# Experts ranked by token count, and two of eight positions cut from 96 to 64 token slots

## The reference, cut to what matters

```
logits = x @ router_w + router_b
top_v, top_i = top_k(logits, 2);  top_p = softmax(top_v)
out = sum over e of gate[:, e] * ((silu(x @ w1[e]) * (x @ w3[e])) @ w2[e])
```

## Time and profile before

| | us |
|---|---|
| median of 3 runs (2125.89 to 2126.81) | 2125.93 |
| span of the profiled execution, first to last instruction | 2121.4 |
| median less the profile's span | 4.5 |
| PE busy in the span | 2007.0 (95%) |
| DVE, ACT, POOL busy | 745.1, 593.2, 53.8 |
| HBM read | 614.43 MB |

### The profile page before, as it was taken

One profiled execution on the slowest core, in us unless ns is written; L12 is line 12 of the kernel. 1 busy time (PEld: TensorE's weight loads), 2 busy tenths in 40 slices (PEclk: granted clock), 3 DMA queues, 4 the chain that ended last, 5 costly groups with the idle time before them and its releaser, 6 DMA issues.

```text
span 2121.4 us, 38539 instructions
## 1 busy us (share of the span) xinstructions
PE 2007.0 (95%) x17128; PEld 1242.4 (59%) x17128; DVE 745.1 (35%) x1325; ACT 593.2 (28%) x972; POOL 53.8 (3%) x96
## 2 busy tenths in 40 slices
PE   9999999987978879999999999999999999999997
PEld 7778874322422237877888877745556554344445
DVE  8775663110100117786444677610001000000015
ACT  6555541000100016565444755400000000000005
POOL 1000000000000000120000002000000000000000
PEclk9999999999999999999999999999999999999999
DMA  9854468999999997254555551389999999999991
GB/s 220 205 157 140 158 218 333 421 421 421 421 421 421 421 408 232 80 169 159 178 181 196 162 178 42 134 309 405 409 412 405 372 405 407 412 409 409 411 409 73
DMA packets 239199, 622.96 MB, mean 294 GB/s; under 512 B 35496, under 2 KB 120360, under 8 KB 201648
## 3 DMA queue, kind: packets, MB, share of 16 engines
q1 hardware_dynamic: 233872, 611.87, 77.0%
q10 hardware_dynamic: 4544, 6.42, 0.8%
q0 software_dynamic: 608, 2.10, 0.3%
HBM read 614.43 MB, written 3.81 MB: 291 GB/s over the span
## 4 chain that ended last, share of the span: by engine, by line
PE 75%; DMA 15%; DVE 5%; ACT 2%; issue 1%; SPq 0%; POOL 0%; DVEq 0%; ACTq 0%; POOLq 0%
PE ps L2840 21%; PE ps L2857 11%; DMA ring<-in_w_gate 8%; DMA ring<-in_w_down 5%; PE ps L664 5%; PE ps L666 5%; PE ps L665 5%; PE ps L2546 4%; PE ps L674 2%; PE ps L675 2%; PE ps L678 2%; PE ps L2561 2%; DMA arena<-in_w_gate 1%; DMA arena<-in_w_down 1%; PE ps L2135 1%
## 5 line engine op out<-in xcount | busy, mean ns | idle before, releaser
L2840 PE MATMUL ps<-ring,arena 128*32 128x512 f32 (+1 forms) x3936 | 395.2, 557 | 0.0
L704 DVE TENSOR_TENSOR ring_parts<-ring,high_parts 128x2048 fp32r<-128x2048 f32 (+2 forms) x117 | 261.9, 2244 | 93.9 <-ACT high_parts L700 93.0
L2840 PEld LDWEIGHTS ps<-ring,arena 128*32 128x32 f32 x3936 | 148.1, 110 | 230.1 <-issue 204.8
L3053 DVE TENSOR_TENSOR arena<-ps,arena 128x768 f32<-128x768 f32 (+1 forms) x24 | 21.4, 891 | 601.6 <-ACT arena L2956 537.5
L700 ACT CAST high_parts<-ring 128x2048 fp32r<-128x2048 f32 (+2 forms) x117 | 217.5, 1862 | 31.7 <-PE ps L666 28.4
L666 PE MATMUL ps<-high_parts,arena_parts 128*128 128x512 f32 (+1 forms) x494 | 194.3, 393 | 0.0
L664 PE MATMUL ps<-high_parts,hT_parts 128*128 128x512 f32 (+1 forms) x472 | 191.6, 406 | 0.0
L665 PE MATMUL ps<-ring_parts,hT_parts 128*128 128x512 f32 (+1 forms) x472 | 185.1, 392 | 0.0
L2857 PE MATMUL ps<-ring,arena 128*32 128x256 f32 x3168 | 176.1, 379 | 0.0
L2956 ACT ACTIVATE arena<-ps,arena 128x256 f32<-128x256 f32 (+1 forms) x72 | 27.6, 454 | 511.8 <-PE ps L2840 511.7
L2546 PE MATMUL ps<-ring,arena 128*64 128x512 f32 x584 | 145.0, 596 | 21.8 <-DMA ring<-in_w_gate 11.9
(11 more groups left out here) (650 smaller groups left out, 2502.7 us busy)
## 6 DMA issues: line engine op xcount, KB each, us to landing
ring<-in_moe_w SPq DMA_DIRECT2D x220, 512.0 KB, 10.0
ring<-in_moe_w SPq DMA_DIRECT2D x66, 1024.0 KB, 12.0
ring<-in_moe_w SPq DMA_DIRECT2D x108, 384.0 KB, 8.2
ring<-in_w_gate SPq DMA_DIRECT2D x39, 1024.0 KB, 27.6
ring<-in_w_down SPq DMA_DIRECT2D x35, 1024.0 KB, 27.6
ring<-in_w_up SPq DMA_DIRECT2D x34, 1024.0 KB, 27.6
ring<-in_w_in SPq DMA_DIRECT2D x104, 256.0 KB, 4.6
arena<-in_w_up SPq DMA_DIRECT2D x26, 1024.0 KB, 26.4
```

The source lines that it names most:

```text
L704: dve.tensor_tensor(low_flat(p), raw_flat(p), f32(high_flat(p)), ALU.subtract).then_inc(split, 1)
L2840: mm = pe.matmul(dst, x_rows, w[:, :, s * n:(s + 1) * n], start=(c == 0), stop=(c == KC - 1), skip_group_check=True)
```

## The change

The experts are ranked by token count on the chip. Expert 0 keeps position 0 and is given rank 1, since its weights are loaded before the router is done. The seven others are put in the other positions by their rank: position 2 takes the second fewest (rank 7), position 7 the fewest (rank 8), and both compute two lots (64 slots) in place of three. The second path is taken when an expert has more tokens than its own slots.

DVE makes the order in a small one-hot matrix `o_turn`, and everything by expert (places, gates) is turned into position order with it. SP waits for `expert_order` before the first piece of position 1, loads the expert's number into a register once for each position, and addresses all weights of positions 1 to 7 by that register.

```diff
 LOTS, SPAN = 3, 96
+LOTS_AT, RANK_AT = (3, 3, 2, 3, 3, 3, 3, 2), (1, 2, 7, 3, 4, 5, 6, 8)
+ROWS_AT_POS = [32 * sum(LOTS_AT[:k]) for k in range(len(LOTS_AT))]
+        def stream_ranked(sp, pieces):
+            expert = {}
+            for p in pieces:
+                if p.free_at:
+                    sp.wait_ge(used, p.free_at)
+                elif p.slot == RAW + 1:
+                    sp.wait_ge(sig("router_psum"), 3)
+                if p.bucket not in expert and p.bucket:
+                    if not expert:
+                        sp.wait_ge(*ended("expert_order"))
+                    at = p.bucket
+                    expert[at] = sp.value_load(order_i[0:1, at:at + 1], min_val=0, max_val=NE2 - 1)
+                sources = p.source(bass.ds(expert[p.bucket], 1)) if p.bucket else [src for _, src in p.copies]
+                for (dst, _), src in zip(p.copies, sources):
+                    sp.dma_start(dst, src).then_inc(piece_ready[p.slot], 16)
...
+        def rank_key_dve(dve):
+            dve.tensor_copy(o_key_base[:], desc[:, 32 - NE2:32])
+            dve.tensor_copy(o_rank_at[:], slot_no[:, 0:NE2])
+            dve.drain()
+            dve.memset(o_key_base[:, 0:1], BIG)
+            for at, r in enumerate(RANK_AT):
+                if r != at + 1:
+                    ins = dve.memset(o_rank_at[:, at:at + 1], float(r))
+            vstep(dve, ins)
+        def ranked_place_dve(dve):
+            upto, total = router_psum(moe2)
+            place = r_place[:, :, 0:NE2]
+            dve.wait_ge(sig("router_psum"), 2 * moe2.number)
+            dve.tensor_copy(place[:, 1], total[:, 0, :])
+            dve.tensor_tensor(place[:, 0], upto[:, 0, :], r_hit[:, 0, 0:NE2], ALU.mult)
+            vstep(dve, dve.scalar_tensor_tensor(out=o_key[:], in0=total[:, 0, :], scalar=float(NE2), in1=o_key_base[:], op0=ALU.mult, op1=ALU.add))
+            dve.tensor_tensor(place[:, 1], place[:, 1], upto[:, 1, :], ALU.add)
+            vstep(dve, dve.scalar_tensor_tensor(out=o_key[:], in0=total[:, 1, :], scalar=float(NE2), in1=o_key[:], op0=ALU.mult, op1=ALU.add))
+            dve.tensor_tensor(place[:, 1], place[:, 1], r_hit[:, 1, 0:NE2], ALU.mult)
+            vstep(dve, dve.tensor_tensor(o_pairs, ..., ALU.is_ge))
+            vstep(dve, dve.tensor_reduce(o_rank[:], o_pairs, AX, ALU.add))
+            vstep(dve, dve.tensor_tensor(o_turn[:], ..., ALU.is_equal))
+            ranked(dve, o_place, place)
+        def ranked(dve, dst, src):
+            for t in range(NT):
+                ins = dve.tensor_tensor(o_wide[:, t], o_turn[:], src[:, t].unsqueeze(1).to_broadcast([P, NE2, NE2]), ALU.mult)
+            vstep(dve, ins)
+            vstep(dve, dve.tensor_reduce(dst, o_wide, AX, ALU.add))
+        def expert_order_dve(dve):
+            ...   (six steps; the fourth signals expert_order, the last two make o_cap, 96 or 64 for each expert)
...
         def router2_dve(dve):
             lower_rows_dve(dve, moe2, 1)
+            rank_key_dve(dve)
             dve.wait_ge(sig("router_psum"), 3)
...
-            place_dve(dve, moe2)
+            ranked_place_dve(dve)
         def gates2_dve(dve):
             yield from two_gates(dve, moe2, NE2)
+            ranked(dve, o_gate[:, :, :, 0], ...)
+            dve.tensor_copy(o_gate[:, :, :, 1], ...).then_inc(sig("moe2_gates"), 1)
...
             def up(st, c):
-                for g in range(LOTS):
+                for g in range(st.lots):
             def down(st, i):
-                    for g in range(LOTS):
+                    for g in range(st.lots):
             def result(b):
-                for g in range(LOTS):
+                for g in range(n):
             def last_result():
-                    for g in range(LOTS):
+                    for g in range(LOTS_AT[b]):
             def silu(st):
-                for g in range(LOTS):
+                for g in range(st.lots):
             def product(st):
-                hid, hidT = wide_hid[:, 0:LOTS * n], wide_hidT[st.no % 2][:, 0:LOTS * n]
+                hid, hidT = wide_hid[:, 0:lots * n], wide_hidT[st.no % 2][:, 0:lots * n]
...
             select(0)
             rows(0)
             hot_kept()
+            expert_order_dve(dve)
             all_of(gates2_dve(dve))
             count_dve(dve, f)
```

More of the change, by code:

```diff
@@ L76 @@
 LOTS, SPAN = 3, 96
+LOTS_AT, RANK_AT = (3, 3, 2, 3, 3, 3, 3, 2), (1, 2, 7, 3, 4, 5, 6, 8)
+LAST = 32 * LOTS_AT[-1]
+ROWS_AT_POS = [32 * sum(LOTS_AT[:k]) for k in range(len(LOTS_AT))]
+FEW = min(r for r, n in zip(RANK_AT, LOTS_AT) if n < LOTS)
+assert all((n < LOTS) == (r >= FEW) for r, n in zip(RANK_AT, LOTS_AT)) and RANK_AT[0] == 1
 PIECE = 2048
@@ L437, in plan_wide @@
                     st.first, st.last = k == 0, c0 + st.n == DFF
+                    st.lots = LOTS_AT[b]
                     f.plan.append(st)
             def down(st):
-                rows = w2[st.bucket][st.c0:st.c0 + st.n].rearrange("(p c) n -> p c n", p=P)
-                return [new_piece([(0, PIECE, rows[:, c:c + 2, :])]) for c in range(0, st.n // P, 2)]
+                rows = w2[0][st.c0:st.c0 + st.n].rearrange("(p c) n -> p c n", p=P)
+                lot = []
+                for c in range(0, st.n // P, 2):
+                    p = new_piece([(0, PIECE, rows[:, c:c + 2, :])])
+                    p.source = lambda e, c0=st.c0, n=st.n, c=c: [
+                        w2[e].rearrange("a n d -> (a n) d")[c0:c0 + n].rearrange("(p c) n -> p c n", p=P)[:, c:c + 2, :]]
+                    p.bucket = st.bucket
+                    lot.append(p)
+                return lot
             slot_flat[RAW:RAW + 2] = [arena[:, WIDE_SLOT:WIDE_SLOT + PIECE], hT[:].rearrange("p c s -> p (c s)")]
@@ L614, in stream_moe @@
                 lot = [p for st in f.plan for pair in st.up + st.down for p in pair]
+                stream(sp, sorted(lot, key=lambda p: p.n))
             else:
                 lot = [p for st in f.plan for p in st.up] + [p for st in f.plan for p in st.down]
-            stream(sp, sorted(lot, key=lambda p: p.n))
+                stream_ranked(sp, sorted(lot, key=lambda p: p.n))
             sp.wait_ge(sig("routed"), 2 * f.number)
@@ L1863, in count_dve @@
             vstep(dve, dve.tensor_tensor(r_count[:, 0:nb], r_count[:, 0:nb], total[:, 1, :], ALU.add))
+            if f is moe2:
+                for at in range(NE2):
+                    dve.memset(o_row_at[:, at:at + 1], float(ROWS_AT_POS[at] - 1 - ROWS_AT_POS[-1]))
+                vstep(dve, dve.tensor_tensor(r_count[:, 0:nb], r_count[:, 0:nb], o_cap[:], ALU.subtract))
+                vstep(dve, dve.tensor_scalar(r_count[:, 0:nb], r_count[:, 0:nb], float(f.cap), float(S), ALU.add, ALU.min))
             vstep(dve, dve.tensor_reduce(r_count[:, 0:1], r_count[:, 0:nb], AX, ALU.max))
@@ L1919, in two_gates @@
                 ins = dve.tensor_tensor(gate[:, t, :, 0:f.e], first, second, ALU.add)
-            ins.then_inc(sig(f"{f.name}_gates"), 1)
+            if f is moe1:
+                ins.then_inc(sig("moe1_gates"), 1)
+            else:
+                vstep(dve, ins)
         def logits_dve(dve, n, bias):
@@ L2859, in down @@
                                            stop=(st.last and j == st.n // P - 1), skip_group_check=True)
-                            if final and (k, g, s) == (1, LOTS - 1, 1):
+                            if final and (k, g, s) == (1, st.lots - 1, 1):
                                 mm.then_inc(sig("moe2_half_done"), 1)
@@ L3151, in rest_dve @@
                     places = r_place[:, :, 0:f.subs]
-                    dve.tensor_scalar(places, places, -float(P if k else f.cap), None, ALU.add).then_inc(m("shifted"), 1)
+                    if f is moe2 and k == 0:
+                        dve.tensor_tensor(places, places, o_cap[:].unsqueeze(1).to_broadcast([P, NT, NE2]), ALU.subtract).then_inc(m("shifted"), 1)
+                    else:
+                        dve.tensor_scalar(places, places, -float(P if k else f.cap), None, ALU.add).then_inc(m("shifted"), 1)
                     dve.wait_ge(*m.at("shifted", k + 1))
```

85 lines of the change are left out of this document (57 added, 28 removed).

## The result

The changed kernel takes 2112.97 us (median of 4 runs, 2110.49 to 2113.52) where the kernel before takes 2125.91 beside it: ratio 0.9939, 95% interval 0.9925 to 0.9953, 12.9 us less. In a second set of runs it took 2114.66 (4 runs) against 2125.03: 0.9948, 0.9931 to 0.9964. The prediction was 8.0 us less, 2117.9. Both medians lie in its range (2112 to 2124); the second lies 0.3 us and the first 2.0 us under the band that it called its forecast (2115 to 2121).

A forecast was written before the change was run, and what follows sets the result against it. PE and the DMAs were both taken as full, the DMAs' lead over PE deciding. Stage -11.1, start +2.5 and branch +0.6 gave -8.0 us: span 2113.4, time 2117.9 with 4.5 around it; range 2112 to 2124.

The forecast's parts named there:

- The bound: Expert stage: PE needs 85.2 us per 96-slot position and the transfers about the same, so both are full.
- The lead, piece by piece: Weights lie ready 12.7 us early at position 2, eaten after some 15 pieces; second gather returns 6 to 8 us.
- The stage, -11.1: Expert stage: lead at the end 5.4, shorter last piece 0.9, fuller queue 4.5, smaller result 0.3 us off.
- The slow stretch: 1640 to 1720, after the second gather: 379 instead of 410 GB/s, 6.0 us lost, 4.5 expected back.
- The start, +2.5: Router to first gather: added DVE steps, 1.6 us for places and 0.9 for keys; bounds 1.5 and 5.
- The branch, +0.6: PE's branch at the stage's end fetches code by DMA behind four queued pieces: 0.6 us longer, bounds 0 and 1.25.
- Gates, order, SP, next stage at nothing: Added gate and order steps hidden, SP's DMAs by register short enough, next stage's weights not late: 0 us.
- The two rules weighed: Skill rules on clock falling to 1.2 GHz in PE pauses (0.84 us here) and on DMA limits, 358 and 435 GB/s.
- rival 4: Clock falls in positions 2 and 7, two-lot piece 3.4 us against 2.56 of DMA: 2119 to 2121; chance 0.24 with another rival.
- The rate: Weight stream at 410 GB/s: by the fabric ceiling of 435 it could still speed up by 6%.

The follow-up runs named there:

- the control: The kernel before itself, unchanged, run again beside the others: 2125.99 us (10 runs), ratio to before 1.0002.

## Why the prediction was right, and where its sizes were off

- **The bound.** Both full, the lead decides: right. With a full queue every trace shows 405 to 413 GB/s over stretches of 60 us and more, whatever PE does; stretches of 20 us go from 391 to 416 in the two traces of the changed kernel.
- **The lead, piece by piece.** Issue, landing and use of every piece stand in the trace of the changed kernel. The lead is 12.6 us where position 2 begins (12.7 forecast) and is gone after 14 pieces of two lots (some 15). The second gather gives back 7.3 us (6 to 8). One step of the path failed: that lead was to last until position 7, for positions 3 to 6 were taken as even. The stream needs 86.1 us for each of them (the first pieces of positions 3 and 7 land at 1622.80 and 1967.10), PE 85.1, so 1.5 us are left when position 7 begins, and PE waits from its second piece on. The sum doesn't feel it, since it takes the whole lead at the end as gone either way. It fits that position 7, cut on top of position 2, adds only 2.6 us of stage.
- **The sum, in the traces.** The first pair is the trace of before and the first of the changed kernel, the second pair the control and its second trace:

| us | forecast | first pair | second pair |
|---|---|---|---|
| ahead of `rstd`, where no edit reaches | 0 | +0.7 | +1.8 |
| start | +2.5 | +3.6 | +3.9 |
| stage | -11.1 | -12.0 | -11.8 |
| branch | +0.6 | -2.1 | -2.2 |
| rest | 0 | +0.1 | -1.5 |
| span | -8.0 | -9.7 | -9.7 |

- **The stage, -11.1.** Within 1 us. The lead and the shorter last piece gave 6.7 (8.16 to 1.49), 6.3 forecast. The slow stretch was taken at 4.5 of 6.0 and its rate came back whole (410 from 1640 to 1720); the last landing, counted from the first up piece, came 5.4 us earlier in the first pair and 5.8 in the second, where 4.8 were forecast with the smaller result. The doubt, that a result's writes slow the stretch in any case, was wrong: with the queue full they don't show in the rate.
- **The start, +2.5.** DVE's part was right (2.1; 0.6 for the keys and 1.5 for the places, 0.9 and 1.6 forecast). What was taken as a bound only, the clock, was there every time: in all ten traces with ranking and nine spare turns a slow spell lies in the gather, 7.3 to 7.8 us to the first up piece, and in neither trace of before (5.8). So the term is 1.1 to 1.4 us short. PE's two pauses had grown, from 0.4 to 1.0 us ahead of the sums and from 0.4 to 1.9 ahead of the gather. That they bring the slow spell is likely, since it left the gather or shrank when they were filled (two traces), but not shown: in the second trace of the changed kernel the clock had fallen before either.
- **The branch, +0.6.** The term with the wrong sign. "It meets a queue" was argued from one pair of durations; the changed kernel has 2.6 us in both traces, 2.1 less than before. Why is open. This error and that of the start partly cancel (-2.7 and +1.1 us), which is luck.
- **Gates, order, SP, next stage at nothing.** Right: the kernel with fixed addresses shows it for the register, and the gates are used at 1395.26, 6 us after they are ready.
- **The two rules weighed.** In the first trace of the changed kernel the clock is 1.00 in both short positions, with PE at 29.67 of 40 us busy. But it fell for a few us in position 7 in five of the ten traces in which that position is short, the second trace of the changed kernel among them (row below), and in none of the four in which it is long. So the condition of rival 4 came about in part, without a price that shows: from first up piece to last landing the two traces of the changed kernel have 678.6 us with the spell and 678.4 without.

```profile
2010.00:2030.00 20.00, 12.97 (x140) 4.04 (x136) 2.23 (x3) 0.84 (x2) 3.62 (x4) 0.91 1.02 414
```

- **The rate.** The Trainium skill's fabric ceiling of 435 GB/s (DMA: Bandwidth & Descriptors, "Specifications") stayed out of reach: 416 is the most that a stretch of 20 us shows in this stage.
- **The measured 12.9.** 9.7 of it is in the traces. The rest is which executions were traced: those of before took 2123.2 and 2124.7 us with a median of 2125.8 over its 56 runs beside the other kernels, those of the changed kernel 2113.5 and 2115.0 with 2113.3. The time before `rstd` alone differs by 2.7 us over 14 traces.

## What to carry to other kernels

When weights stream beside an engine that is also full, work taken from the engine is worth what it lets the transfers do. Look for stretches where the rate is under its best value and save the work in or ahead of them: position 0, where PE never waited, was worth 8.2 us of stage on top of positions 2 and 7 (in a kernel that leaves out tokens), position 7 on top of position 2 only 2.6. Ranking the experts costs 2.1 us of small steps and, here, 1.5 to 1.9 more in a gather at a lower clock; filling PE's pauses ahead of it took most of that away. And take a code jump at a stage's end from a trace of the new program, not from the old one.

## What the runs showed of the hardware

- In three traces with PE as the only pace the stage takes 691.90 to 691.91 us from first piece to last; in six where the DMAs set the pace it is 679.9 to 681.7. A stream that is the bound brings its own scatter of 1 to 2 us.
- PE's granted clock fell for a few us in position 7 in five of ten traces with two lots there, where PE waits up to 2 us for a piece, and in none of four with three lots. It cost nothing that the stage shows (680.1 us with it, 679.9 without).
- An issue on SP lasts 0.33 us with room in the queue and up to 3.2 us without, with a fixed address as with a register.
- A TensorE branch of 0.46 to 6.29 us at the same place of nearly the same program.
